# Seven steps moved in the hand-written order of a hybrid decoder trunk

## The reference, cut to what matters

```python
for l in range(DEPTH):                       # DEPTH = 2
    x = x + 0.5 * swiglu(rms_norm(x, ffn1_norm[l]), ...)
    h = rms_norm(x, mix_norm[l])
    (dq, dk, dv, iq, ik, iw, gq, gk, gv, gz, ga, gb, mq) = split_columns(h @ w_in[l])
    out_a = dsa_attention(...)     # 6 heads x 64; an indexer of 8 heads x 32 picks 128 keys for each query
    out_b = gdn_mixer(...)         # 6 heads x 64, causal conv of width 4, chunked delta rule, chunk 64
    out_c = memory_attention(...)  # 4 heads x 64 over 256 memory tokens
    x = x + jnp.concatenate([out_a, out_b, out_c], axis=-1) @ w_out[l]
    x = x + 0.5 * swiglu(rms_norm(x, ffn2_norm[l]), ...)
```

## Time and profile before

| | |
|---|---|
| median of three runs | 2092.73 us (2092.61 to 2092.9) |
| the profiled execution: its own time | 2092.73 us |
| its span, first to last instruction | 2090.9 us |
| TensorE busy | 2074.3 us, 99% of the span |
| VectorE, ScalarE, GpSimd busy | 49%, 37%, 18% |
| chain that ended last | PE 89%, DVE 6%, ACT 3%, POOL 1%, issue 1% |

### The profile page before, as it was taken

One profiled execution on the slowest core, in us unless ns is written; L12 is line 12 of the kernel. 1 busy time (PEld: TensorE's weight loads), 2 busy tenths in 40 slices (PEclk: granted clock), 3 DMA queues, 4 the chain that ended last, 5 costly groups with the idle time before them and its releaser, 6 DMA issues.

```text
span 2090.9 us, 31663 instructions
## 1 busy us (share of the span) xinstructions
PE 2074.3 (99%) x13097; PEld 1678.5 (80%) x13097; DVE 1027.8 (49%) x1391; ACT 774.6 (37%) x1058; POOL 380.4 (18%) x343
## 2 busy tenths in 40 slices
PE   9999999999999999999999999999999999999999
PEld 7888888877777888888888888888777778888887
DVE  5433333588775643333333443336887765343322
ACT  5222222475556422222232222224755554222211
POOL 1010011205034511001111110111050444101000
PEclk9999999999999999999999999999999999999999
DMA  5222222322121222222222222223212112222222
GB/s 194 88 98 100 96 91 96 122 81 82 43 92 39 99 86 99 100 96 91 99 99 100 100 92 90 104 82 136 81 63 74 61 61 81 100 100 97 92 98 76
DMA packets 30645, 192.40 MB, mean 92 GB/s; under 512 B 3216, under 2 KB 5392, under 8 KB 11984
## 3 DMA queue, kind: packets, MB, share of 16 engines
q1 hardware_dynamic: 30160, 189.80, 26.0%
q10 hardware_dynamic: 384, 1.14, 0.1%
HBM read 188.70 MB, written 2.10 MB: 91 GB/s over the span
## 4 chain that ended last, share of the span: by engine, by line
PE 89%; DVE 6%; ACT 3%; issue 1%; POOL 1%; DMA 0%; SPq 0%; DVEq 0%; ACTq 0%; POOLq 0%
PE psum L995 28%; PE psum L997 27%; PE psum L996 27%; PE psum L1475 1%; PE psum L1425 1%; DVE wl L1916 1%; PE psum L1442 1%; ACT wh L1542 1%; PE psum L1313 1%; PE psum L1310 1%; DVE wrk L2014 1%; DVE XL L1931 1%; DVE m L2012 1%; DMA raw<-weights 0%; PE psum L1131 0%
## 5 line engine op out<-in xcount | busy, mean ns | idle before, releaser
L995 PE MATMUL psum<-XH,wh 128*128 128x512 f32 x1904 | 754.9, 396 | 5.6 <-DVE XL L1876 2.3
L997 PE MATMUL psum<-XH,wl 128*128 128x512 f32 x1904 | 742.3, 390 | 0.0
L996 PE MATMUL psum<-XL,wh 128*128 128x512 f32 x1904 | 742.2, 390 | 0.0
L995 PEld LDWEIGHTS psum<-XH,wh 128*128 128x128 f32 x1904 | 357.5, 188 | 102.0 <-issue 22.4
L997 PEld LDWEIGHTS psum<-XH,wl 128*128 128x128 f32 x1904 | 357.6, 188 | 74.9
L996 PEld LDWEIGHTS psum<-XL,wh 128*128 128x128 f32 x1904 | 357.8, 188 | 71.6 <-issue 1.0
L1924 DVE TENSOR_TENSOR wl<-raw,wh 128x2048 fp32r<-128x2048 f32 x88 | 201.8, 2293 | 159.4 <-ACT wh L1547 159.4
L1542 ACT ACTIVATE wh<-raw 128x2048 fp32r<-128x2048 f32 (+1 forms) x88 | 161.6, 1836 | 305.2 <-PE psum L997 305.0
L995 PE MATMUL psum<-HH,wh 128*128 128x512 f32 x704 | 274.1, 389 | 0.0
L996 PE MATMUL psum<-HL,wh 128*128 128x512 f32 x704 | 274.0, 389 | 0.0
L997 PE MATMUL psum<-HH,wl 128*128 128x512 f32 x704 | 274.0, 389 | 0.0
(11 more groups left out here) (255 smaller groups left out, 1939.7 us busy)
## 6 DMA issues: line engine op xcount, KB each, us to landing
raw<-weights SPq DMA_DIRECT2D x143, 1024.0 KB, 4.8
raw<-weights SPq DMA_DIRECT2D x32, 896.0 KB, 4.4
xT<-xt SPq DMA_DIRECT2D x4, 512.0 KB, 6.2
memT<-memt SPq DMA_DIRECT2D x2, 1024.0 KB, 4.8
out<-xT SPq DMA_DIRECT2D x8, 256.0 KB, 5.0
stripsA<-strip_table SPq DMA_DIRECT2D x2, 768.0 KB, 6.7
raw<-weights SPq DMA_DIRECT2D x2, 512.0 KB, 6.7
stripsB<-strip_table SPq DMA_DIRECT2D x2, 512.0 KB, 7.3
```

The lines of the kernel that those rows point to most:

```text
L995: pe.matmul(out_ap, a_hi, b_hi, start=first, stop=False)
L996: pe.matmul(out_ap, a_hi, b_lo, start=False, stop=False)
L997: return pe.matmul(out_ap, a_lo, b_hi, start=False, stop=last)
```

## The change

Only the order is changed; no instruction is added or taken out, and no size is changed.

```diff
-FILLED = [s for s in RECURRENCE if s[0] in ("r1", "oc") or s == ("r2", 0, 0)]
+FILLED = [s for s in RECURRENCE if s[0] in ("u", "r1", "oc") or s == ("r2", 0, 0)]
...
-        ev = [("rd",) + g[:1] + (c,) + g[1:] for g in groups[:lead] for c in OUT_ORDER[:3]]
+        ev = [("rd",) + g[:1] + (c,) + g[1:] for c in OUT_ORDER[:3] for g in groups[:lead]]
...
-    for slot, part, k0 in ((8, "lo", 0), (9, "hi", KD // 2), (11, "lo", KD // 2)):
+    for slot, part, k0 in ((8, "hi", 0), (9, "lo", 0), (10, "hi", KD // 2), (12, "lo", KD // 2)):
         per_slot[slot].insert(0, (part, 18, k0, k0 + KD // 2))
-    per_slot[7].append(("hi", 18, 0, KD // 2))
...
-    late = [[], ["mem4", "gate2"], [("idx", 0)], [("idx", 1)], [], [("idx", 2), "gate5"], [],
+    late = [[], ["mem4", "gate2"], [("idx", 0)], [("idx", 1)], [], [("idx", 2), "gate5"], [("idx", 3)],
             ["gate7", "silu_qk"], []]
...
         ev(name, c)
-        if n == 7:
-            put(("idx", 3))
         put(("tap", n), ("conv", n))
...
-                    later.append((int((name, c) == ("dk", 1)), ("sq", nj)))
+                    later.append((0, ("sq", nj)))
...
-            pull(0.98 if step != ("r1", 0, 0) else 1.96)
+            pull(0.98)
...
             put(("hi", 16, 0, KD // 2), ("hi", 16, KD // 2, KD), ("ev", N_GROUPS - 1), ("lo", 16, 0, KD // 2),
-                ("gsplit", 0), ("lo", 16, KD // 2, KD), ("hi", 17, 0, KD // 2), ("gsplit", 1))
+                ("lo", 16, KD // 2, KD), ("gsplit", 0), ("hi", 17, 0, KD // 2), ("gsplit", 1))
...
-            sel((0, 0, 1, 1, 2, 2, 1, 1)[slot] if slot < 8 else 0)
+            sel((0, 0, 0, 2, 2, 2, 1, 1)[slot] if slot < 8 else 0)
```

## The result

| | before | changed |
|---|---|---|
| median of four runs each | 2092.81 us (2092.61 to 2092.9) | 2106.24 us (2105.45 to 2108.29) |
| the profiled execution: its own time | 2092.73 us | 2104.53 us |
| its span | 2090.9 us | 2102.7 us |

The account below looks back on a forecast made before the run. TensorE, busy 2074.3 of 2090.9 us, was taken to bound the kernel, so new waits add to the end. Terms of 5.05 us a layer, +10.1 for two, gave 2102.8, stated as 2102.5 us; range 2096.5 to 2106.5.

Parts of the forecast that it names:

- part 1: Index scores: `sq0` delayed 2.9 us against 1.1 slack, head sums wait; +1.85 us a layer, bounds 1.5 to 1.95.
- part 2: Start of the recurrence: `sq14` in front of the `WT` copies makes `u` wait; +0.55 us a layer.
- part 3: Recurrence: `U` now behind `ev dk2` makes `r2 0 0` wait, +0.8 us; two waits at `r1` go, -1.6.
- two waits of `r1` go: Recurrence: TensorE's waits in front of `r1`, 0.9 us for `St` and 0.7 us for `osq`, go in each layer.
- parts 2 and 3 together: Recurrence: new waits less the removed ones, -0.25, say -0.3 us a layer; bounds -0.9 to +0.3.
- parts 4 to 6: Slots 2 and 3: `gsplit 0` ends late behind a half split that meets GpSimd's rounding; +1.0 us a layer, upper bound 1.5.
- part 7: Slot 9: half `lo 18`, split behind `att 9` on VectorE, comes late; +2.5 us a layer, bounds 1.4 to 3.2.
- the sum: One layer: 1.85 - 0.3 + 1.0 + 2.5 = 5.05 us; two layers: +10.1 us.
- the 0.1 of the lower bound: Slot 2: with the shortest durations, `gsplit 0` comes only 0.1 us late for TensorE.
- one or both large waits don't come: Rivals: `sq0`, the split of unit 18, or both in time; one 0.17 (2097.8 to 2099.1 us), both 0.09 (2094.1).
- the freed VectorE wins: Rival: splits moved out of the way of `St` and `comb`; 4.4 us less, 2088.3 us; chance 0.05.
- More collisions: Rival: each later split or product meets GpSimd as well; over 2106.6 us; chance 0.07.

Follow-up runs that it names:

- the kernel that does only this: Kernel before, with second half of `lo 15` in front of `r1 1 0`, `ap14` and `ap15` one gap later: 2089.72 us against 2093.01.
- The pair of runs on part 4: Kernel before with second half of `lo 16` in front of `gsplit 0`: 2095.53 us; same with GpSimd's rounding held until both `gsplit`s done: 2093.51 us; against 2093.02.

## Why the prediction was right, and where it fell short

| step of the prediction, one layer | predicted, us | measured, us |
|---|---|---|
| part 1, head sums wait for the squares | +1.85 | +2.0 and +2.1 (shift); wait 1.5 |
| part 2, `u` waits for `WT` | +0.55 | +0.5 (shift); wait 0.4 |
| part 3, `r2 0 0` waits for `U` | +0.8 | +0.8 (shift); wait 0.7 |
| part 3, two waits of `r1` go | -1.6 | -1.65, in the kernel that does only this |
| parts 2 and 3 together | -0.3 | -0.35 in each layer; alone the same (shift) |
| parts 4 to 6, slot 2 | +1.0 | +1.24 and +1.23 (shift) |
| part 7, slot 9 | +2.5 | +2.2 (shift, layer 1); wait 2.9 |
| the sum | +5.05 | +5.1 (the terms above) |
| a fall of the clock after slot 9 | no term | +1.4 to +1.6 |

- **Every wait came at the place and for the instruction named.** The method that gave them is the same each time: the slack of an input against the delay of its queue. Part 1 is the plainest case, 1.1 us of slack against 2.9 us of delay. That the sum of the terms is met to 0.1 us is in part luck: parts 1 and 4 were taken 0.2 us too low each and part 7 0.3 too high.
- **Part 1** lies above its upper bound of 1.95. The prediction let the four matmuls of `idx 3` cost a tenth and put that inside the wait. They cost 0.2 to 0.3 us, and in front of the wait, so it adds up.
- **Parts 4 to 6** were a little low. The value rests on the second half of `lo 16` starting at the end of the rounding and lasting 1.1 us, and it did; `gsplit 0` was ready 0.2 us later than I let it. A likely reason is that the two `gsplit`s lie beside GpSimd's next work as well (1.48 us for both, 1.29 where GpSimd is still); no run tests this one. The pair of runs on part 4 shows the exclusion; without it part 4 costs 0.25, not the 0.1 of the lower bound.
- **The step that failed is the sum**: it prices a wait at its length alone. A wait of 2.9 us also lets the clock fall to 1.2 GHz in many executions, and the work behind it then runs at half speed for some 3 us. One fall costs 1.5 us by the row (3.1 us of work at half speed) and 1.4 to 1.6 by the shifts of three traces. In the profiled execution the terms (2 x 5.1) and one fall make 11.6 of the 11.8 us. By this estimate an execution with two falls takes near 2106 us, where the median of the four runs lies; its mean clock is 0.998, as in the trace without part 1, which had two. No trace shows that the median run had just these two. The prediction had looked only at the mean clock of before, which had no wait of this length in the mixers.
- **The range** was said to take in all bounds, but their sum is 2106.6 and the range ends at 2106.5. Nothing in it allows for the clock. That it holds the median of 2106.24 is luck: it was made wide for collisions and overlaps, and 3.4 us of another origin just fitted in.
- **The rivals.** That one or both large waits don't come is excluded by the list of waits. That the freed VectorE wins is excluded too, though its parts were real: the 1.6 us for `r1` and the wait for `pT` can be had, in other orders. More collisions: the time does lie near that rival's, over 2106.6 in four of thirteen executions, but the list of waits of the profiled one has no more of them than were named.
- Why a wait of 2.9 us is followed by a fall in some executions and layers and not in others stays open: of the six in the three traces that have it, four were. So does what happened in the runs at 0.997, which have no trace.

## What to carry to other kernels

Before you move a step in a list that all engines share, work out for each engine what is queued behind it and with how much slack TensorE picks that up; of 2.9 us of delay, 1.1 us of slack took off 1.1 here, and the rest was lost. When TensorE's waits are summed, add the clock: where it fell, a pause of some three microseconds cost half of itself again here, while none of those of 0.7 to 1.5 us in the mixers was followed by a fall. And put a VectorE step with two SBUF inputs where GpSimd does not read SBUF: of the 1.25 us of part 4, 1.0 came from the neighbour on GpSimd and not from the step's own length.

## What the runs showed of the hardware

- More matmuls made the kernel faster: nine in each layer, put into a pause of 2.9 us, took the median from 2105.45 (of thirteen; 2106.24 of four) to 2102.96 us, because the granted clock stayed at 1.00 behind it, where it had fallen to 0.51 in many executions.
- Waits of 1.5 us (`nsq`, six in three traces) and 1.2 us (slot 2, ten in five traces) were not followed by a fall in any trace. Those of 2.9 us were followed by one in four cases of six, and those of 2.0 to 2.3 us at the start of the launch in two of four.
- The fall need not come in the pause: it began 0.35 us before the end of the wait in one case, and 0.1, 0.3 and 1.1 us behind it in the others, with TensorE at work again. It covered 3.1 to 3.4 us of work each time.
- Where a split on VectorE and a rounding on GpSimd meet, they take turns, whole instructions at a time: 3.17 us for two splits and one rounding, 2.33 us for the two splits alone.
